# Slabs of the mLSTM heads on two pairs of PSUM banks, the sample group ahead of the reciprocal, later gate activations, and earlier far factors in the GLA stage

## The reference, cut to what matters

```
hp  = rms_norm(x, gain)
all = hp @ rec_w_in            # q, k, v, output gate of 4 mLSTM heads; q, k, v, gate of 4 GLA heads; small gates
per mLSTM head, in chunks:
  s   = (q k') * exp(intra - m)
  num = w_inter * (C q) + s v
  den = w_inter * (n q) + sum(s)
  h   = num / max(|den|, exp(-m))
  C, n = decay * (C, n) + weighted sums over the chunk
hm  = rms_norm(h, m_norm_g) * sigmoid(output gate)
hg  = rms_norm(gla(q, k, v, log_a), g_norm_g) * silu(gate)
x   = x + [hm, hg] @ rec_w_out ; then norm, ConvFFN; layer 1: differential attention, ConvFFN
```

## Time and profile before

| | |
|---|---|
| runs | 1443.25, 1444.33, 1450.47 us; median 1444.33 |
| profiled execution | 1447.93 us, its span 1446.4 us |
| busy: TensorE, VectorE, ScalarE, GpSimd | 95%, 58%, 36%, 8% of the span |
| TensorE's granted clock, mean | 0.977 |
| mLSTM heads, with the first slabs beside them | about 54 to 245 us |
| GLA stage and output projection | about 245 to 357 us |

### The profile page before, as it was taken

One profiled execution on the slowest core, in us unless ns is written; L12 is line 12 of the kernel. 1 busy time (PEld: TensorE's weight loads), 2 busy tenths in 40 slices (PEclk: granted clock), 3 DMA queues, 4 the chain that ended last, 5 costly groups with the idle time before them and its releaser, 6 DMA issues.

```text
span 1446.4 us, 28921 instructions
## 1 busy us (share of the span) xinstructions
PE 1380.3 (95%) x11458; PEld 1319.3 (91%) x11458; DVE 842.9 (58%) x1274; ACT 525.4 (36%) x856; POOL 110.9 (8%) x158
## 2 busy tenths in 40 slices
PE   5899899989999999999999999997999999999997
PEld 4899899879999999999999787884999999999997
DVE  5455458746766666632344888888456666664221
ACT  4433435435233233322234556564342332232110
POOL 0211112102000000000100000000110000000000
PEclk9999999879999999999999999997999999999999
DMA  5655464212322232322224787873222222233320
GB/s 205 121 133 89 160 147 107 76 47 73 98 92 87 88 100 87 123 93 87 78 77 176 206 284 209 290 228 112 74 88 89 100 87 88 100 104 111 114 75 22
DMA packets 46937, 170.86 MB, mean 118 GB/s; under 512 B 6206, under 2 KB 7534, under 8 KB 46618
## 3 DMA queue, kind: packets, MB, share of 16 engines
q1 hardware_dynamic: 38506, 143.61, 29.3%
q0 software_dynamic: 8368, 26.38, 9.0%
HBM read 158.45 MB, written 11.51 MB: 118 GB/s over the span
## 4 chain that ended last, share of the span: by engine, by line
PE 85%; DVE 6%; ACT 3%; issue 3%; DMA 3%; POOL 1%; DVEq 0%; ACTq 0%; POOLq 0%
PE ps L523 56%; PE ps L574 13%; PE ps L695 2%; PE ps L920 1%; PE ps L950 1%; PE ps L935 1%; DMA e_negm<-gate_rows 1%; ACT w_hi L1166 1%; PE ps L884 1%; PE ps L923 1%; DMA qb<-q_rows 1%; PE ps L929 1%; PE ps L1053 1%; DVE s_prod L2195 1%; PE ps L737 1%
## 5 line engine op out<-in xcount | busy, mean ns | idle before, releaser
L1664 DVE TENSOR_TENSOR w_lo<-raw,w_hi 128x1024 fp32r<-128x1024 f32 (+1 forms) x189 | 244.6, 1294 | 378.0 <-ACT w_hi L1166 378.0
L523 PE MATMUL ps<-h_hi,w_hi 128*128 128x260 f32 x1616 | 459.4, 284 | 5.6 <-DVE h_lo L1673 4.3
L523 PE MATMUL ps<-h_hi,w_lo 128*128 128x260 f32 x1616 | 457.7, 283 | 0.0
L523 PE MATMUL ps<-h_lo,w_hi 128*128 128x260 f32 x1616 | 456.2, 282 | 0.0
L523 PEld LDWEIGHTS ps<-h_hi,w_hi 128*128 128x128 f32 x1616 | 305.2, 189 | 7.9 <-issue 4.6
L523 PEld LDWEIGHTS ps<-h_lo,w_hi 128*128 128x128 f32 x1616 | 305.1, 189 | 0.1
L523 PEld LDWEIGHTS ps<-h_hi,w_lo 128*128 128x128 f32 x1616 | 305.2, 189 | 0.0
L1166 ACT CAST w_hi<-raw 128x1024 fp32r<-128x1024 f32 (+1 forms) x189 | 208.2, 1102 | 222.4 <-PE ps L523 216.3
L523 PE MATMUL ps<-a_lo,w_hi 128*128 128x260 f32 x704 | 199.0, 283 | 0.0
L523 PE MATMUL ps<-a_hi,w_hi 128*128 128x260 f32 x704 | 198.7, 282 | 0.0
L523 PE MATMUL ps<-a_hi,w_lo 128*128 128x260 f32 x704 | 198.7, 282 | 0.0
(11 more groups left out here) (391 smaller groups left out, 2061.9 us busy)
## 6 DMA issues: line engine op xcount, KB each, us to landing
raw<-in_w_ffn SPq DMA_DIRECT2D x88, 512.0 KB, 3.6
raw<-in_w_down SPq DMA_DIRECT2D x32, 704.0 KB, 4.0
k_pages<-in_cache_k SPq DMA_DIRECT2D x32, 512.0 KB, 5.6
v_pages<-in_cache_v SPq DMA_DIRECT2D x32, 512.0 KB, 7.2
raw<-in_w_rec_in SPq DMA_DIRECT2D x29, 512.0 KB, 6.6
raw<-in_w_att_kv SPq DMA_DIRECT2D x24, 512.0 KB, 4.9
raw<-in_w_rec_out SPq DMA_DIRECT2D x8, 512.0 KB, 4.0
raw<-in_w_att_q SPq DMA_DIRECT2D x8, 512.0 KB, 3.6
```

What stands on the lines that cost most here:

```text
L523: ins = TE.matmul(half(bank, h), w_part[:, buf, w], m_part[:, k_at + k, h * HALF:(h + 1) * HALF], start=start, stop=stop)
L1664: V.tensor_tensor(w_lo[:, n % 2, 0:nk * P], raw[:, n % RAW, 0:nk * P], w_hi[:, n % 2, 0:nk * P].bitcast(F32), ALU.subtract).then_inc(lo_sp ...
```

## The change

The last square of the first norm is added by VectorE as well, and TensorE sums only `ssum`. `summed` thereby counts one more, and the waits on it elsewhere are renumbered with the same meaning.

In the heads the parts use banks 2, 2, 4, 2, 4, 4 (and the bank above each) in place of 2 throughout. `dens` moves from bank 6 to bank 7 and waits for `abs`, `ssq` moves from bank 4 to 2, and the waits for banks are set to match. A quarter of part 2 moves ahead of the chunks, and none is left behind the last one. On VectorE `rec_split(1)` moves behind the second state update, and the sample group moves ahead of the maximum and the reciprocal. On ScalarE `rec_step(first + 1)` moves ahead of the gate activations, and the silu moves from head 2 to head 3.

In the GLA stage of pair 1 VectorE's order changes: far exponents and key exponents ahead of the drain of block 4, far factors ahead of `mixes(0)`, the drain of block 5 ahead of `lows(0)` and `end_factors(1)`. ScalarE does `far_decays(1)` ahead of `roots(0)`.

```diff
+        PART_BANK = (2, 2, 4, 2, 4, 4)
...
             def norm(bank):
 
-                pe.wait_ge(summed, KT - 1)
+                pe.wait_ge(summed, KT)
                 for h in range(2):
-                    TE.matmul(half(bank, h), ONES, ssum[:, h * HALF:(h + 1) * HALF], start=True, stop=False)
-                pe.wait_ge(squared, KT)
-                for h in range(2):
-                    ins = TE.matmul(half(bank, h), ONES, sq[:, (KT - 1) % 2, h * HALF:(h + 1) * HALF], start=False, stop=True)
+                    ins = TE.matmul(half(bank, h), ONES, ssum[:, h * HALF:(h + 1) * HALF], start=True, stop=True)
                 ins.then_inc(nP.sem, 1)
...
                 def part(j, k0=0, k1=KT):
                     n = first + j
                     if k0 == 0:
-                        pe.wait_ge(drained, n)
-                    slab_part(n, n % 2, range(k0, k1), 2)
+                        if j == 2:
+                            wait(pe, mA, "vt", h)
+                        elif j:
+                            pe.wait_ge(drained, (0, n, 0, n - 1, n - 1, n)[j])
+                        elif h:
+                            wait(pe, mA, "rms", h - 1)
+                    slab_part(n, n % 2, range(k0, k1), PART_BANK[j])
...
                 else:
-                    wait(pe, mA, "abs", h - 1)
+                    wait(pe, mA, "abs_s", h - 1)
...
                 part(0)
-                if h:
-                    wait(pe, mA, "rms", h - 1)
+                pe.wait_ge(drained, first)
...
                 part(1)
+                part(2, 0, 2)
                 wait(pe, mD, "p", h)
...
-                    part(2, 2 * c, 2 * c + 2)
+                    if c < NC_M - 1:
+                        part(2, 2 * c + 2, 2 * c + 4)
...
+                wait(pe, mA, "abs", h)
                 wait(pe, mD, "nq", h)
-                TE.matmul(ps[:, 6, 0:B], ONES, nq[:, :], start=True, stop=True).then_inc(mP.sem, 1)
+                TE.matmul(ps[:, 7, 0:B], ONES, nq[:, :], start=True, stop=True).then_inc(mP.sem, 1)
                 part(4)
                 wait(pe, mA, "sq", h)
                 wait(pe, mD, "kv", h)
                 for n in range(2):
-                    ins = TE.matmul(half(4, n), ONES, sq[:, 0, n * HALF:(n + 1) * HALF], start=True, stop=True)
+                    ins = TE.matmul(half(2, n), ONES, sq[:, 0, n * HALF:(n + 1) * HALF], start=True, stop=True)
...
+                rec_step(first + 1)
                 act.wait_ge(drained, first + 1)
-                gate = (z[:, 12:14, :], z[:, 14, :], z[:, 15, :], None)[h]
-                if gate is not None:
+                if h < M_HEADS - 1:
+                    gate = (z[:, 12:14, :], z[:, 14, :], z[:, 15, :])[h]
                     S.activation(gate, gate, ACT.Sigmoid)
-                if h == 2:
+                else:
                     S.activation(z[:, 24:28, :], z[:, 24:28, :], ACT.Silu)
-                if gate is not None:
-                    S.preload_act_table_set(LN_EXP)
-                rec_step(first + 1)
+                S.preload_act_table_set(LN_EXP)
...
+            far_decays(1)
             roots(0)
-            far_decays(1)
...
-            for c in range(KT - 1):
+            for c in range(KT):
                 add_squares(dve, V, 0, c)
...
                 rec_split(0)
-                rec_split(1)
                 for c in range(NC_M):
+                    if c == 2:
+                        rec_split(1)
...
-            early_drain(4, 0)
             exponents(1, "far", 0, 2)
             key_exponents(1)
+            early_drain(4, 0)
+            factors(1, "far", 0, 2)
             mixes(0)
-            factors(1, "far", 0, 2)
+            early_drain(5, 0)
             lows(0)
             end_factors(1)
-            early_drain(5, 0)
```

More of the change, by code:

```diff
@@ L343, in build @@
         mA = Steps(sem("mlstm_act"), "ws wi e kt vt en abs abs_s sq lr rms")
-        mD = Steps(sem("mlstm_dve"), "em qw ve p cn0 cn1 cn2 cn3 nend den rden h vw kw nw ns nq kv cs cq hs dn rd hs2 t mix")
+        mD = Steps(sem("mlstm_dve"), "em qw ve p cn0 cn1 cn2 cn3 nend vw kw nw ns nq den rden h kv cs cq hs dn rd hs2 t mix")
         hA, hD = Steps(sem("mlstm_out_act"), "hi"), Steps(sem("mlstm_out_dve"), "lo")
@@ L533, in first_slab @@
                 multiply(name, h_hi, h_lo, 0, 0, 0, 0, KT - 1, True, False, ready, signal=False)
-                pe.wait_ge(summed, KT * r + KT - 1)
+                pe.wait_ge(summed, KT * r + KT)
                 for g in range(2):
@@ L678, in _ @@
             pe.wait_ge(drained, S_REC_IN - 1)
-            slab_part(S_REC_IN - 1, (S_REC_IN - 1) % 2, range(KT // 2), 2).then_inc(early_free, 1)
+            slab_part(S_REC_IN - 1, (S_REC_IN - 1) % 2, range(KT // 2), 4).then_inc(early_free, 1)
             wait(pe, lD, "z0")
@@ L682, in _ @@
             v_chunks(0)
-            slab_part(S_REC_IN - 1, (S_REC_IN - 1) % 2, range(KT // 2, KT), 2)
+            slab_part(S_REC_IN - 1, (S_REC_IN - 1) % 2, range(KT // 2, KT), 4)
             def early(m, bank, step=1):
@@ L1170, in square @@
                 if c >= 2 or not isinstance(i, int) or i:
-                    act.wait_ge(summed, 2 * i + (max(KT * r - 1, 0) + c - 1))
+                    act.wait_ge(summed, 2 * i + (KT * r + c - 1))
                 xc = x[:, 2 * i + c, :] if isinstance(i, int) else x[:, ds(2 * i + c, 1), :].rearrange("p o t -> p (o t)")
@@ L1221, in rec_step @@
                 out = gates[:, :] if REC_TILES[n] == 28 else z[:, REC_TILES[n], :]
-                bank = 2 * (n % 4) if n < len(FIRST_SLABS) else 2
+                bank = 2 * (n % 4) if n < len(FIRST_SLABS) else PART_BANK[(n - len(FIRST_SLABS)) % PER_HEAD]
                 S.copy(two(out), pair(bank)).then_inc(drained, 1)
@@ L1321, in _ @@
                 wait(act, mP, "dens", h)
-                S.activation(den_s[:, :], ps[:, 6, 0:B], ACT.Abs).then_inc(mA.sem, 1)
+                S.activation(den_s[:, :], ps[:, 7, 0:B], ACT.Abs).then_inc(mA.sem, 1)
                 if h == M_HEADS - 1:
@@ L1330, in _ @@
                 wait(act, mP, "ssq", h)
-                rsqrt(two(rstd[:, :]), pair(4), P, mA, "lr", h).then_inc(mA.sem, 1)
+                rsqrt(two(rstd[:, :]), pair(2), P, mA, "lr", h).then_inc(mA.sem, 1)
                 if h < M_HEADS - 1:
@@ L1653, in add_squares @@
             else:
-                eng.wait_ge(summed, max(KT * r - 1, 0) + c)
+                eng.wait_ge(summed, KT * r + c)
                 ops.tensor_tensor(ssum[:, :], ssum[:, :], sq[:, c % 2, :], ALU.add).then_inc(summed, 1)
@@ L1894, in _ @@
                 V.tensor_copy(n_end[:, h:h + 1], c_n[:, P:P + 1]).then_inc(mD.sem, 1)
-                wait(dve, mA, "abs", h)
-                V.tensor_tensor(den[:, :], den[:, :], e_negm[:, :], ALU.max).then_inc(mD.sem, 1)
-                wait(dve, mD, "den", h)
-                V.reciprocal(den[:, :], den[:, :]).then_inc(mD.sem, 1)
-                rec_split(2)
-                wait(dve, mD, "rden", h)
-                V.tensor_tensor(h_head[:, 0:T], ps[:, 6, :], den[:, :], ALU.mult).then_inc(mD.sem, 1)
                 V.scalar_tensor_tensor(out=v_ws[:, :], in0=v[:, T:NT], scalar=K_SCALE, in1=w_s[:, 2, :], op0=ALU.mult,
@@ L1911, in _ @@
                 V.tensor_tensor(nq[:, :], n_s[:, h, :], q[:, T:NT], ALU.mult).then_inc(mD.sem, 1)
+                wait(dve, mA, "abs", h)
+                V.tensor_tensor(den[:, :], den[:, :], e_negm[:, :], ALU.max).then_inc(mD.sem, 1)
+                wait(dve, mD, "den", h)
+                V.reciprocal(den[:, :], den[:, :]).then_inc(mD.sem, 1)
+                rec_split(2)
+                wait(dve, mD, "rden", h)
+                V.tensor_tensor(h_head[:, 0:T], ps[:, 6, :], den[:, :], ALU.mult).then_inc(mD.sem, 1)
                 dve.wait_ge(kb_in, 16 * (h + 1))
```

## The result

The changed kernel takes 1432.26 us (median; 1426.34 to 1445.0), the kernel before, measured beside it, 1445.52 (1441.46 to 1451.45). The ratio is 0.9907, 95% interval 0.9890 to 0.9925: 13.4 us less (10.8 to 15.9), where 12.7 were forecast. The profiled execution took 1437.28 us, its span 1435.7.

The account below looks back on a forecast made before the run. TensorE was taken to bound the kernel, 85% of the chain that ended last. Norm -0.7, heads -8.5 and GLA -3.5 sum to -12.7 us: median 1431.6 us, 0.9% less, with 80% for 1425 to 1439.

Parts of the forecast that it names:

- The norm: Input norm: an eighth VectorE add (+0.8) replaces two TensorE matmuls (-1.51) on the chain; -0.7 us, bounds 0 and -1.0.
- TensorE's side of the heads: mLSTM heads: chunk 3's state 10.8 us after the head's point, then VectorE's chain of 14.3; 25.1 us per head.
- TensorE waits some 2 us: Heads, ahead of the sum of squares: TensorE ready at 12.1 us, VectorE's chain at 14.3; 1.2 in head 3.
- The heads' sum: Four mLSTM heads together: 108.9 us before, 100.4 after; -8.5 us, nearly all from heads 0 and 2.
- The GLA term: GLA stage: VectorE's new order removes TensorE's whole wait for x ahead of the far levels; -3.5 us, bounds 0 and -3.5.
- rival (c): GLA stage: the gap moves rather than vanishes, by late mixes or the half clock; 1435 us; chance 11%.
- Rival (d): GLA stage: the slow clock shrinks once its idle time is gone; up to 5 us more, 1427 us; chance 9%.
- The clock: TensorE's granted clock in the heads: waits of 2 us should not lower it; nothing taken, about 1.7 us each otherwise.
- Rival (b): Heads: the waits of 2 us bring the clock down once per head; 6.8 us back, 1438 us; chance 11%.
- Rival (f): Heads: the clock, once down at the sum of squares, stays down; 20.8 us lost, 1452.4 us; chance 4%.
- The forecast's sign of being wrong: Wrong if the sum-of-squares wait is near zero or over 3 us, clock falls within heads, or the GLA gap reappears.
- (e): Heads: VectorE's chain doesn't bind, TensorE runs through at 12.1 us; 4 x 2.2 us more, 1423 us; chance 3%.

Follow-up runs that it names:

- x_norm: Only the first norm's change (eighth add on VectorE) made to the kernel before; 1446.06 us, ratio 1.0006.
- a_short: Changed kernel with the samples' product with the query done for one of eight samples only, VectorE's chain 1.07 us shorter; 1431.58 us, ratio 0.9881 to the kernel before.
- a_order: Changed kernel with VectorE's sample group put back behind the reciprocal and its product; 1431.06 us, ratio 0.989 to the kernel before.
- a_onebank: Changed kernel with all parts of the heads in one pair of banks again, orders as changed; 1433.9 us, ratio 0.9907 to the kernel before.
- x_gla: Only the GLA order changed against the kernel before, norm and heads as before; 1440.14 us, ratio 0.9956.
- a_guard: Changed kernel with GpSimd's multiply of the samples' state held back until the low split of part 2 is done; 1430.26 us, ratio 0.9916 to the kernel before.
- after2: The changed kernel again, unaltered, in a second session; 1434.77 us, ratio 0.9936 to the kernel before.
- a_coll: Changed kernel with GpSimd's multiply held back to start together with VectorE's v_end; 1433.7 us, ratio 0.9928 to the kernel before.
- b_act: Kernel before with one edit: ScalarE's drain and cast of part 1 stand ahead of the gate activations; 1440.72 us, ratio 0.9966.
- x_heads: Only the mLSTM heads changed against the kernel before, norm and GLA as before; 1440.18 us, ratio 0.9966.
- after: The changed kernel in its first session and profile, all edits against the kernel before; 1432.26 us, ratio 0.9907.
- g2: Changed kernel with part 5 in banks 0 and 1, work filling the wait ahead of the squares, and GpSimd's multiply held back; 1426.28 us, ratio 0.9852 to the kernel before.
- g3: g2 with VectorE's reciprocal done by ScalarE as the exponential of minus the logarithm; 1422.16 us, ratio 0.9845 to the kernel before.

## Why the prediction held

**The norm** was -0.7: shown, 0.65, in x_norm's profile; its time alone (+0.9 us, -1.6 to 3.2) shows neither sign.

**TensorE's side of the heads.** The forecast had 25.1 us from the head's point to the sum of squares, the same in all four; it is 25.0 in all four, in six profiles with VectorE's chain whole and the two bank pairs. The reasoning that VectorE's chain takes over (13.59 us from `c_n` to the square; 13.49 measured) and that the sample group and the banks count for nothing there is shown by a_short, a_order and a_onebank. "TensorE waits some 2 us" was 1.7 and 1.2; the low split ahead of part 4 makes it wait 0.68 first, not 0.4. The silu in head 3 cost nothing.

**The heads' sum was sized too high**: -8.5, measured -4.9 (2.5 to 7.4). Two steps of it failed.

First, 108.9 us for the heads before is one profile, in which head 0 took 29.9, and its wait of 3.8 us was put down to the sigmoid ahead of the drain. In front of both, ScalarE waited for the row of `e_negm`, and TensorE's wait goes with that one: 3.80 us beside 3.9 in this profile, 2.04 beside 2.1 in x_norm, 0.23 beside 0.3 in x_gla, with the same sigmoid in all three. In the first two the clock fell behind it as well, 1.7 us each. So head 0 takes 29.9, 28.4 and 25.6 us in three executions of the same order, and the four heads 108.9, 107.5 and 105.6. (The new order takes the row off the path: in a_order it is 5.4 us late and head 0 takes 25.0.)

Second, "nothing waits in it", said of the 20.11 us between the heads, and "the transposes cover part 0's drain" left out what stands ahead of part 1 and of the low split of part 2: ScalarE's exponentials wait for rows (1.6 us in head 0 in this profile), and GpSimd's multiply can hold VectorE (1.3 in head 2, 0.2 in head 3). The 0.5 us by which the low split comes earlier had been written down as sufficient. Between the two first profiles the account closes: the heads are 8.9 us shorter (108.9 to 100.1), 1.8 are lost ahead of head 0's point and 1.8 between the heads, and the last sum of squares comes 5.3 us earlier besides the norm's 0.65 (237.08 - 231.13 = 5.95).

**The GLA term came out larger than counted**: -3.5, measured -6.4, with an interval (2.9 to 9.7) that doesn't exclude -3.5. The profiles show more than the wait. It went as counted, and rival (c) had no part. Rival (d) came true in part, for the far levels: in all ten profiles with the new order at least their first six steps take 0.44 us, in all four with the old one they take 0.65 from the second on, some 1.7 us. The whole stretch, 33.8 to 35.3 us with the old order, the wait of 3.5 in it, is 29.2 to 29.6 at a clock of 0.82 to 0.83, 27.7 at 0.88 (a_guard), and 25.7 to 25.8 where the clock stays at 1.00 (after2, a_coll, a_onebank). What decides between these in one order of instructions stays open; no run changed that alone.

**The clock was the open flank.** The forecast took nothing for it in the heads, because 2.63 us in head 2 of the profile before left it at 1.00. That was one execution. In x_gla, with the heads as before, the same wait in head 2 (2.65 us) was followed by 0.72 over 163 to 169, and head 2 took 29.0 us against 28.1. The clock also fell behind waits of 2.04 (x_norm), 2.83 (b_act) and 3.67 us (a_short), and not behind 1.97 (x_heads), 2.63 (a_guard) and 2.65 us (x_norm, head 2). Rival (b) came true in head 3 alone: behind its wait of 1.24 us the clock fell in two of five profiles (after, x_heads), 1.7 us each, and never behind the 1.7 us of heads 0 to 2 in the same five. Rival (f) did not: the fall cost 1.7 us and not 5.2. The forecast's sign of being wrong, a fall within the heads, thus came at their very end, in this kernel's own first profile. (e) is refuted by the waits for the square.

**How much of the 12.7 was luck.** The errors of the two large terms, +3.6 and -2.9, nearly cancelled. The three parts timed alone make 10.4 us (0.9 more for the norm, 4.9 and 6.4 less), and the changed kernel 13.4 and, repeated, 9.3; the intervals allow all of these. And the forecast counts waits, where part of the gain is clock: over the timed runs the mean granted clock of a whole execution is 0.985 for the changed kernel and 0.979 for the kernel before (beside x_norm), which is 21 us lost against 30 ((1 - clock) x time). The difference of 9 us is an upper bound, an estimate, since a low clock costs nothing while TensorE is idle; the forecast had 1.7. Of the 20 runs of the changed kernel the six fastest (1426.3 to 1430.6 us) have a clock of 0.988 to 0.989, and the nine at 0.982 to 0.984 take 1431.4 to 1445.0.

## What to carry to other kernels

When a wait is taken from the engine that sets the time, work out the next engine's chain from the same starting event to the same meeting point: the difference of the two is what is gained, and here it said within 0.1 us where each head would end. Before a difference from one profile is booked as a saving, ask which of its parts hang on a DMA's landing or on the granted clock behind a wait; those differ from execution to execution and need a second profile. When the clock is read over a stage, let the window reach past the last wait: here the fall came 1 us behind the point where the stage had been cut off. A wait that can't be removed can be filled: a quarter of a slab in banks that were idle took 1.4 us of wait out of each of three heads, where the second pair of banks is worth about 1 us in the gap between two heads.

## What the runs showed of the hardware

- VectorE's `v_end` of 0.28 us took 1.92 to 1.95 when GpSimd's multiply of 1.9 us started beside it (after, a_coll, a_short), and at most 0.29 in a_guard and g2 and 0.40 in g3, where this was kept away.
- The same small rows by DMA, in kernels that are alike up to there but for the norm, let ScalarE wait 3.4 to 8.3 us in different executions.
- Behind a wait of TensorE in the heads the granted clock fell to 0.50 in some executions and not in others: with 2.65 us in x_gla and not with 2.65 in x_norm, in the same head and order; with 1.24 us in after and x_heads and not in after2, a_coll and a_guard. A fall cost 1.7 us (0.72 over 6 us), in g3 3.4 (0.57 over 8 us).
- The same instructions from the near levels of pair 1 to the late matmuls took 29.4 us at a mean clock of 0.83 and 25.7 at 1.00.
